# Hybrid decoder layer on one core: the mixed stage ordered by half steps and costs, two heads ahead, the softmax partly on ScalarE

## The reference

```python
def decoder_layer(x, ...):
    z = x @ w_in + b_in                      # u, q, k, v, two gates
    ssm = glu(gelu(s5_scan(u)))              # 32 groups, 64 states each
    att = attention(rope(q), rope(k), v) @ w_attn_up   # window 128, 8 heads, 2 kv heads, sinks
    mix = (sigmoid(g_ssm) * ssm + sigmoid(g_attn) * att) @ w_out
    x1 = layer_norm(ALPHA * x + mix)
    return layer_norm(ALPHA * x1 + peer(x1))

def peer(x):                                 # 8 heads, 16384 experts
    q = x @ peer_wq                          # per head two halves of 64
    v1, i1 = top_k(q[..., 0] @ k1.T, 16)     # 128 keys a side
    v2, i2 = top_k(q[..., 1] @ k2.T, 16)
    sc, sel = top_k(v1[:, None] + v2[None, :], 16)     # 16 of 256 sums
    idx, gate = (i1 * 128 + i2)[sel], softmax(sc)
    h = einsum('nhkd,nd->nhk', peer_u[idx], x)         # 128 rows of 1024 for each token
    return einsum('nhk,nhkd->nd', gelu(h) * gate, peer_v[idx])
```

## Time and profile before

| | us |
|---|---|
| median of 3 runs (lowest, highest) | 2155.72 (2154.64, 2161.78) |
| the profiled execution, and its span | 2155.55, span 2153.7 |
| first gather asked for | 346.0 |
| first dot product of tile 2 | 1033.75 |
| busy over the span: PE, DVE, POOL, ACT | 1588.6, 1368.6, 1335.9, 386.0 |
| mean granted TensorE clock | 0.88 of full speed |
| moved by DMA | 675.05 MB, 313 GB/s over the span |

### The profile page before, as it was taken

One profiled execution on the slowest core, in us unless ns is written; L12 is line 12 of the kernel. 1 busy time (PEld: TensorE's weight loads), 2 busy tenths in 40 slices (PEclk: granted clock), 3 DMA queues, 4 the chain that ended last, 5 costly groups with the idle time before them and its releaser, 6 DMA issues.

```text
span 2153.7 us, 16271 instructions
## 1 busy us (share of the span) xinstructions
PE 1588.6 (74%) x4705; PEld 794.3 (37%) x4705; DVE 1368.6 (64%) x3118; ACT 386.0 (18%) x905; POOL 1335.9 (62%) x1370
## 2 busy tenths in 40 slices
PE   6979986776987786876649676767658676777776
PEld 4667853443544433321224222223223222222222
DVE  7551237878999799758766675754648655444444
ACT  1222211123223222001111111111102121111111
POOL 0064004646686656676767777777777777777664
PEclk9979998868998898998879898889889898999889
DMA  5243335957899998999889999999999999999997
GB/s 216 88 82 115 135 115 208 374 196 282 315 401 378 385 343 308 373 356 346 297 342 351 358 378 347 377 365 381 356 389 344 351 362 388 377 356 397 350 361 294
DMA packets 186553, 675.05 MB, mean 313 GB/s; under 512 B 20961, under 2 KB 23441, under 8 KB 186049
## 3 DMA queue, kind: packets, MB, share of 16 engines
q0 software_dynamic: 167056, 609.25, 75.7%
q1 hardware_dynamic: 17632, 59.51, 7.7%
q10 hardware_dynamic: 1776, 5.24, 0.6%
HBM read 669.71 MB, written 3.69 MB: 313 GB/s over the span
## 4 chain that ended last, share of the span: by engine, by line
PE 29%; POOL 25%; DVE 16%; issue 15%; DMA 10%; another core or an unknown queue 3%; ACT 2%; SPq 0%; ACTq 0%; DVEq 0%; POOLq 0%
PE bank L812 12%; POOL region L525 9%; POOL wring L518 7%; PE bank L743 6%; POOL region L518 6%; DMA region<-in_pv,region 3%; PE bank L764 2%; DVE region L1238 2%; DMA wring<-in_pu,region 2%; DMA small<-in_pv,region 2%; POOL wring L525 1%; DVE wring L1238 1%; PE bank L564 1%; PE bank L783 1%
## 5 line engine op out<-in xcount | busy, mean ns | idle before, releaser
L812 PE MATMUL bank<-region,small 128*128 128x512 f32 (+1 forms) x1296 | 658.9, 653 | 293.4 <-ACT small L1482 146.3
L525 POOL DMA_INDIRECT region<-in_pv,region x392 | 441.5, 1126 | 219.7 <-issue 101.8
L812 PEld LDWEIGHTS bank<-region,small 128*128 128x128 f32 (+1 forms) x1296 | 247.7, 202 | 687.6 <-issue 530.9
L1238 DVE CUSTOM_DVE_ANT_0 wring<-wring,region 128x1024 f32<-128x1024 f32 x286 | 347.7, 1226 | 235.4 <-DMA wring<-in_pu,region 197.3
L1238 DVE CUSTOM_DVE_ANT_0 region<-region 128x1024 f32<-128x1024 f32 x290 | 353.1, 1226 | 189.2 <-DMA region<-in_pu,region 156.5
L518 POOL DMA_INDIRECT region<-in_pu,region x290 | 324.0, 1117 | 210.8 <-DVE region L1197 91.5
L518 POOL DMA_INDIRECT wring<-in_pu,region x286 | 300.7, 1051 | 95.3 <-issue 85.6
L1482 ACT ACTIVATE small<-small,region 128x128 f32<-128x128 f32 (+1 forms) x480 | 155.4, 387 | 652.3 <-DVE region L1212 294.3
L812 PE MATMUL bank<-discretisation,small 128*128 128x512 f32 (+1 forms) x196 | 111.1, 695 | 104.4 <-issue 53.3
L812 PE MATMUL bank<-wring,small 128*128 128x512 f32 x256 | 123.4, 615 | 24.4 <-issue 17.2
L743 PE MATMUL bank<-xT,wring 128*128 128x192 f32 (+1 forms) x512 | 130.5, 416 | 0.0
(11 more groups left out here) (246 smaller groups left out, 1712.7 us busy)
## 6 DMA issues: line engine op xcount, KB each, us to landing
wring<-in_w SPq DMA_DIRECT2D x102, 512.0 KB, 4.3
region<-in_pv,region POOLq DMA_INDIRECT x392
region<-in_pu,region POOLq DMA_INDIRECT x290
wring<-in_pu,region POOLq DMA_INDIRECT x286
out_y<-region ACTq DMA_DIRECT2D x4, 512.0 KB
small<-in_small ACTq DMA_DIRECT2D x1, 1669.0 KB, 14.3
xT<-in_xT SPq DMA_DIRECT2D x1, 1536.0 KB, 20.1
region<-in_x SPq DMA_DIRECT2D x3, 512.0 KB
```

The costliest lines, as they stand in the source:

```text
L525: pool.indirect_dma_start(ring_v[v_at.place[q]], None, io["pv"], bass.IndirectOffsetOnAxis(ind[:, k:k + 1], 0)).then_inc(g_v[v_at.place[q] ...
L812: last = mm(bank[6 + hf][0:tn, :], diag[:, d % DIAGS, 0:tn], ring_v[v_at.place[q]][:, 512 * hf:512 * hf + 512], start=k == 0, stop=t not i ...
L1238: V.tensor_tensor_reduce(out=ring_u[u_at.place[q]], in0=ring_u[u_at.place[q]], in1=x1[t], scale=1.0, scalar=0.0, op0=ALU.mult, op1=ALU.add ...
```

## The change

The same computation in another order. (1) `schedule()` gives each kind of item a cost on VectorE and TensorE (`COST`) and places the entries of the mixed stage by accumulated cost over the first 176 slots (`SPREAD`), between single slots; tile 0's entries have their own places at slots 50 to 112. A `peer` item is a *half step* of two slots (GELU stays at four). The same walk decides which V rows VectorE adds: those at which its summed load is under TensorE's. By my reading of the costs these are 62 rows of 192, six of them among the first 48. (2) Tile 1's choices are heads 0-1, 2-3 and 4-7. The queries of heads 0 and 1 are computed for tile 1 alone (`wqf`) before tile 0's norm, and for tile 0 later (`wql`); their two weight blocks are loaded ahead into two V places. (3) Items are split: gates into `gs` and `ga`, `wo` by halves with the norm as `ln`, `choose` into `choose` and `index`, the softmax into `s` and `p`, and `pt` apart from `pv`. VectorE and ScalarE do the mixer's items one half step later (`behind_next_step`). (4) The subtraction becomes the exponential's bias and the scaling a copy with a scale, head by head on ScalarE; a second buffer holds the other kv head's scores. (5) GpSimd's requests of V run on over a tile's end, and lag 6 slots in tiles 1 and 0; before slot 72 there are seven U places instead of eight. (6) SP's stop for slot 72 and the loads of x stand at the sixth gate's block.

```diff
-U_PLACES = ([0, 1, 2, 3, 4, 5, 10, 11], [0, 1, 2, 3, 10, 11], [0, 1, 2, 3] + list(range(6, 12)))
+U_PLACES = ([0, 1, 2, 3, 4, 5, 10], [0, 1, 2, 3, 10, 11], [0, 1, 2, 3] + list(range(6, 12)))
 V_PLACES = ([0, 1, 2, 3, 4, 5, 6, 7, 8], [0, 1, 2, 3, 4, 5], [0, 1, 2, 3, 4, 5] + list(range(9, 15)))
-V_LAG = 4
-V_SHARE = {1: [1] * 3 + [3] * 3 + [6] * 10, 0: [6] * 3 + [3] * 2 + [0] * 3}
-TOPS_AT = (9, 10, 12, 14, 16, 18, 20, 22, 24, 25)
-LATE_AT = 1
+V_LAG = {1: 6, 0: 6, 2: 4, 3: 4, 4: 4}
+SPREAD = 176
+CHOSEN_FROM, CHOSEN_TO = 50, 112
+COST = {"top": (5.0, 0), "choose": (4.6, 0), "index": (5.0, 0), "sc": (0, 2.5), "s": (4.1, 1.0), "p": (2.8, 0), "pt": (0, 1.4),
+        "pv": (0.4, 1.6), "qkv": (2.4, 10.3), "turn": (0, 1.2), "gs": (0, 5.5), "ga": (0, 5.5), "merge": (2.2, 8.2), "wo": (0.7, 7.0),
+        "ln": (6.2, 0), "xt": (0, 1.3), "wq": (0.3, 5.5), "fold": (0, 0), "wait": (4.0, 0)}
+DOT, V_BY_VECTOR, V_BY_TENSOR = 1.31, 1.29, 1.95
 DIAGS = 8
 STEP_SLOTS = 4
+HALF_STEP = 2
+CHOICES = {1: [(0, 2), (2, 4), (4, 8)]}
+AHEAD = 2
+AHEAD_PLACES = 7
...
+    s += [("wo", 1, 0), ("wo", 1, 1), ("ln", 1), ("wo", 0, 0), ("xt", 1)] + [("wqf", h) for h in range(AHEAD)] + [("sc", 1, 0), ("wo", 0, 1)]
+    s += [("top", 1, 0), ("top", 1, 1), ("choose", 1, 0), ("index", 1, 0), ("ln", 0), ("xt", 0)] + [("wql", h) for h in range(AHEAD)]
+    s += [("wq", 0, 2), ("wq", 0, 3), ("sc", 1, 1)] + [("wq", 0, h) for h in range(4, 8)]
...
+    cost = lambda entry: sum(sum(COST[i[0]]) for i in entry)
+    rate = sum(cost(e) for e in mix + tops) / SPREAD
+    slots, placed, d_load, p_load, on_vector = 0, 0.0, 0.0, 0.0, set()
+    for t in ORDER[:2]:
+        for c in range(n_slots(t) // HALF_STEP):
             s.append(("peer", t, c))
             if c == 0 and t != ORDER[0]:
+                s.append(("final", ORDER[0]))
+                d_load += 8.7
+            for k in range(HALF_STEP * c, HALF_STEP * c + HALF_STEP):
+                slots += 1
+                d_load += DOT
+                entries = []
+                if tops and slots >= CHOSEN_FROM + (CHOSEN_TO - CHOSEN_FROM) * (12 - len(tops)) // 11:
+                    entries.append(tops.pop(0))
+                while mix and placed + sum(map(cost, entries)) + cost(mix[0]) / 2 <= rate * slots:
+                    entries.append(mix.pop(0))
+                for entry in entries:
+                    placed += cost(entry)
+                    d_load += sum(COST[i[0]][0] for i in entry)
+                    p_load += sum(COST[i[0]][1] for i in entry)
+                    s += entry
+                if k and d_load + V_BY_VECTOR < p_load + V_BY_TENSOR:
+                    on_vector.add((t, k))
+                    d_load += V_BY_VECTOR
+                else:
+                    p_load += V_BY_TENSOR
+        s.append(("last", t))
...
+def behind_next_step(items, kinds):
+    out, held, begun = [], [], False
+    for item in items:
+        begun = begun or item[0] == "peer"
+        if begun and item[0] in kinds:
+            held.append(item)
+        elif item[0] == "peer":
+            out += [item] + held
+            held = []
+        elif item[0] in ("last", "final"):
+            out += held + [item]
+            held = []
+        else:
+            out.append(item)
+    return out + held
...
+            asked = 0
+            for q in range(len(on_dve)):
+                u_row(q)
+                while asked + V_LAG[place(asked)[0]] <= q:
+                    v_row(asked)
+                    asked += 1
+            for q in range(asked, len(on_dve)):
+                v_row(q)
...
-            def softmax(n, scores, sink, width, st):
-                mx, ex, sm, rs = (stat[:, 8 * i:8 * i + width] for i in range(4))
+            def softmax_begin(scores, sink, width, st):
+                mx, ex = (stat[:, 8 * i:8 * i + width] for i in range(2))
                 step(V.tensor_reduce(mx, scores, AX, ALU.max))
                 step(V.tensor_tensor(mx, mx, sink, ALU.max))
                 step(V.tensor_tensor(ex, sink, mx, ALU.subtract))
-                V.tensor_tensor(scores, scores, mx.unsqueeze(2).broadcast_to([128, width, st]), ALU.subtract).then_inc(scored, 1)
+                V.tensor_scalar(mx, mx, -1.0, None, ALU.mult).then_inc(scored, 1)
+            def softmax_end(n, scores, width, st):
+                ex, sm, rs = (stat[:, 8 * i:8 * i + width] for i in range(1, 4))
                 dve.wait_ge(expd_s, n)
                 step(V.tensor_reduce(sm, scores, AX, ALU.add))
                 step(V.tensor_tensor(sm, sm, ex, ALU.add))
-                step(V.reciprocal(rs, sm))
-                V.tensor_tensor(scores, scores, rs.unsqueeze(2).broadcast_to([128, width, st]), ALU.mult).then_inc(probs, 1)
-                dve.wait_ge(probs, n)
+                V.reciprocal(rs, sm).then_inc(inverse_s, 1)
+                dve.wait_ge(inverse_s, n)
...
-                step(S.activation(stat[:, 8:8 + width], stat[:, 8:8 + width], ACT.Exp))
-                S.activation(scores, scores, ACT.Exp).then_inc(expd_s, 1)
+                S.activation(stat[:, 8:8 + width], stat[:, 8:8 + width], ACT.Exp)
+                for i in range(width):
+                    last = S.activation(scores[:, i, :], scores[:, i, :], ACT.Exp, bias=stat[:, i:i + 1])
+                last.then_inc(expd_s, 1)
+            def scaled(n, scores, width):
+                act.wait_ge(expd_s, n)
+                act.wait_ge(inverse_s, n)
+                for i in range(width):
+                    last = S.activation(scores[:, i, :], scores[:, i, :], ACT.Copy, scale=stat[:, 24 + i:25 + i])
+                last.then_inc(probs, 1)
...
-                if p == (1, "wo", 0):
+                elif p in ahead:
+                    wait_item(sp, ("ht",))
+                if p == (1, "gs", 5):
```

More of the change, by code:

```diff
@@ new lines, in schedule @@
+    for n in range(1, len(parts)):
+        attention.append([("pt", *parts[n - 1]), ("p", *parts[n])])
+        attention.append([("pv", *parts[n - 1])] + ([("s", *parts[n + 1])] if n + 1 < len(parts) else []))
+    attention += [[("pt", *parts[-1])], [("pv", *parts[-1])]]
+    mix = [first[0], attention[0], first[1], first[2], attention[1], first[3]]
+    first, attention = first[4:], attention[2:]
+    for n, entry in enumerate(attention):
+        mix.append(entry)
+        if n < len(first):
+            mix.append(first[n])
@@ new lines, in schedule @@
+        s.append(("last", t))
+    assert not mix and not tops
+    late = [("top", 2, h) for h in range(4, 8)] + [("choose", 2, 1), ("index", 2, 1)]
+    for t in ORDER[2:]:
+        nxt = [("sc", t + 1, 0), ("sc", t + 1, 1)] + [("top", t + 1, h) for h in range(4)] + [("choose", t + 1, 0), ("index", t + 1, 0)]
+        nxt += [("top", t + 1, h) for h in range(4, 8)] + [("choose", t + 1, 1), ("index", t + 1, 1)]
+        for c in range(n_slots(t) // HALF_STEP):
+            s.append(("peer", t, c))
+            if c == 0:
+                s.append(("final", ORDER[ORDER.index(t) - 1]))
+            if late and c >= 2 and c % 2 == 0:
@@ L125, in mixer_first @@
             held = item
-            out.append(("before", *item[1:]))
         else:
@@ L532, in _ @@
-                for k in range(ns - V_LAG, ns):
-                    v_row(k)
+                for p, (h0, h1) in enumerate(choices(t)):
+                    if t and k == TOPK * h0:
+                        pool.wait_ge(idx_s, chosen(t, p))
+                if u_at.before[q] is not None:
+                    pool.wait_ge(dots, u_at.before[q] + 1)
+                elif u_at.place[q] == 10:
+                    pool.wait_ge(filled, plan.filled[plan.last_use[[p for p in pieces if not p[0] and slot_of[p] == 6][-1]]])
+                elif u_at.place[q] == 11:
+                    pool.wait_ge(filled, plan.filled[("pt", 3, 1, 1)])
```

394 lines of the change are left out of this document (216 added, 178 removed).

## The result

The changed kernel is slower. In runs on one chip it takes 2185.61 us (median of 4 runs, 2179.59 to 2195.67), the kernel before 2158.75 (4 runs, 2154.64 to 2164.22): ratio 1.0139, 95 % interval 1.0094 to 1.0185. Forecast were 2088 us and a gain. The profiled execution took 2180.1 us, span 2177.9.

A forecast was written before the change was run, and what follows sets the result against it. The last three tiles were taken as a gather stream only fewer bytes could shorten, so the change could move only tile 2's first dot. 318 + 179 + 221 + 254 + 1116 = 2088 us, 67 less; range 2050 to 2135.

The forecast's parts named there:

- First gather at 312, first dot at 318: Start of tile 1: two heads searched and chosen ahead, first gather at about 312 instead of 346 us, first dot 318.
- Slots 0 to 47, 179 us: First 48 slots: 145 us of VectorE work, 18 of start waits, a tenth lost; 179 instead of 199 us.
- A V row then sits unused for two slots less: Tiles 1 and 0, V lag six: freed V places against one U place less; nothing taken for either.
- Slots 48 to 111, 221 us: 80.7 MB at 381 GB/s are 212 us; 221 taken, bounds 206 and 240, instead of 206.6.
- Slots 112 to 191, 254 us: Rows and 17 blocks at 375 GB/s are 247 us; 254 taken, bounds 247 and 277, instead of 277.
- a named wait of 10 us: End of the mixed stage: GpSimd's 9.95 us idle until tile 2's indices are written goes, indices due by slot 176.
- Tiles 2 to 4, 1116 us: Last tiles: V requests run over the tile's end, 6 us less; 1116 us, bounds 1108 and 1135.
- The wait of the final norm: Later tile boundaries: norm waits some 8 us longer, covered by ten U places; uncovered, 8 us at each of two boundaries.
- TensorE as the bound: Rival 3, mixed stage: 34 more V rows on TensorE; 2125 us at clock 0.87, 2170 at 0.80; slower has chance 0.09.
- Slots 48 to 191 over 500 us: Sign that the prediction is wrong: these slots take over 500 us with TensorE over 90 % busy.
- TensorE over 90 % busy: Second half of that sign: TensorE over 90 % busy while slots 48 to 191 take over 500 us.
- as coupled as now: Rival 1, mixed stage: only the head start is kept, stage stays at 334 GB/s, ends 34 us earlier; 2121 us, chance 0.14.

The follow-up runs named there:

- lag, drain and spread mended: Changed kernel with V lag of four, tile 0's second output projection drained just before its norm, entries over 190 slots instead of 176 (also called the fastest version): 0.9951.
- Taking work away: Changed kernel, tiles 1 and 0, with half of each V product's columns (TensorE): 1.0054; half of each dot product's elements (VectorE): 1.001; both: 0.9963.
- lag four and moved drain: Changed kernel with V asked for four slots behind U and tile 0's second output projection drained just before its layer norm: 1.0038 of the kernel before.
- the wider spread: Entries over 190 slots instead of 176: alone on the changed kernel 1.0171; with V lag of four and tile 0's second output-projection drain just before its norm 0.9951.
- the old share: 96 of 192 V rows on VectorE instead of 62, on the version with lag, drain and spread mended: 1.0047.
- half the work on both engines: Changed kernel with half the columns of V products on TensorE and half the elements of dot products on VectorE in tiles 1 and 0: 0.9963.
- the mends: Changed kernel with V lag of four and tile 0's second output projection drained just before its norm: 1.0038; with entries over 190 slots too: 0.9951.
- V lag of four: Changed kernel with V requested four slots behind U in tiles 1 and 0 instead of six: 1.0102 of the kernel before on the same chip.

## Why the prediction was wrong, point by point

- **First gather at 312, first dot at 318** (321.3, 326.1). The parts were right (two searches and a choice of two heads from 304.1 to 320.4, 16.3 us against 9.9 + 7.3). What failed is the claim that the search follows the scores: VectorE's in-order queue had a drain of later TensorE work ahead of it, 7 us. With it moved the gather is at 314 to 315, the first dot at 320 to 321. The item list, which was there to be read, showed it.
- **Slots 0 to 47, 179 us** (187.4). VectorE's work was forecast at 145 us and was 139; its waits were larger. With lag, drain and spread mended it is 172.
- **"A V row then sits unused for two slots less... I take nothing for either."** This step weighed the wrong two things. The places that the lag frees are real (V waits 79.0 to 23.4 us) and brought no time, and one U place less cost nothing (0.9997). What it left out is that the later request makes VectorE wait for V rows (12 to 45 us) and, in a circle, GpSimd for dot products (30.5 to 157). The nothing in the sum was nearly right all the same, because these waits took the place of others: 0.4 % in the kernel before, at the edge of its interval, and 0.3 to 0.5 % in the changed one, inside the intervals.
- **Slots 48 to 111, 221 us** (235.3; 229.2 in the fastest version, within the bounds 206 to 240). More TensorE work was foreseen, a pace of 381 GB/s was not reached: 327 GB/s, and 342 in the fastest version. VectorE waited 21 us for TensorE here, before not at all.
- **Slots 112 to 191, 254 us** (299.1). The largest error, and the step that failed. I divided the bytes by 375 GB/s, which puts the engines' waits for each other at nothing, and removed a named wait of 10 us. The wait did go (1.30 us before tile 2's first dot), the pace was never there: 307 GB/s, DMA share 0.85. The old order ran here at 334 GB/s with VectorE's longest wait 3.5 us; the new one has waits of 9.6 to 13.9 us at drains and V rows. In sum VectorE is idle for 92 us instead of 54, and 34 of these are waits for TensorE, which were 0. Its slots 144 to 167 hold the queries' blocks and 16 of VectorE's V rows, and take 101 us instead of 67. No edit mended the stretch: 284 to 316 us in all versions of the new order that compute everything. Taking work away gives 8 us (TensorE), 16 (VectorE), 24 (both).
- **Tiles 2 to 4, 1116 us** (1132.2, before 1121.8). Six us less were forecast for requests that run over the boundary. The changed kernel's slots 192 to 255 took 199 and 200 us, before 192. Versions with lag four and moved drain took 186 to 189, but 200 with the wider spread and the old share on top, and two versions with lag six took 191 and 192. So these slots show no effect of the requests either way. The same instructions took 1098 to 1133 us from tile 2's first to the last dot, so most of the 16 us can't be assigned. The wait of the final norm, priced at 8 us, shows as 15.3 and is covered.
- **The rivals.** TensorE as the bound was to decide below a clock of 0.82; the stages show 0.86 to 0.95, and still it was slower. "Slots 48 to 191 over 500 us" came true (534), "TensorE over 90 % busy" did not (430 of 534, 80 %). At the mean clock of 0.90 these 430 us are an estimated 387 at full clock, against the rival's 401: the work was sized well, and the waits, put at a tenth, were a fifth. The rival that the coupling eats more than the head start brings was missing: apart from TensorE as the bound, I had let the stage stay "as coupled as now" at worst. The chance of 0.09 for slower rested on that bound, so it is no credit to the forecast that slower was among the outcomes.

What stays open: why the last stretch doesn't fall below 274 us with half the work on both engines. Left are the serial chain (last merges, output projection, norm, queries, scores, search), in which TensorE stands for the norm and then VectorE for the queries, and the fixed order in which VectorE meets it; no run separated these two. Also open is why the wider spread pays only behind the mends: the two kernels that show it differ in lag and drain both. That late V rows use up the slack it makes fits (38 us of waits for them in slots 112 to 191, against 9), but was not tried by itself.

## What to carry to other kernels

With in-order engines, look for each moved item at what stands ahead of it in *every* engine's list, before summing busy times; here that was 7 us at once. A request put later to free a buffer moves the wait to the one who uses the data, and here it only took the place of another wait of the same engine: a large wait in a profile is no price until a run without it is faster. The sum of an engine's idle time, by what ended it, says more than one row; here it pointed at the handovers from TensorE, which no single edit removed. A stretch at 99 % DMA share is a result of an order, not a property of the stage: don't multiply bytes of a new order by it. And an edit can gain only in company (the spread), so mend the others before judging it.

## What the runs showed of the hardware

Chips differ in the gather stream. On one of them the last tiles ran at 1035 to 1048 us instead of 1098 to 1133, all four kernels tried on it alike, and the kernel before took 2076.47 us on it against 2157 to 2172 in the other five groups of runs. From 1700 to 1900 us, first that chip (V lag of four), then the usual (changed kernel), GB/s in 40 slices of 5 us:

```profile
GB/s 410 410 410 407 407 408 409 408 406 411 410 410 331 306 340 377 375 327 412 415 406 411 405 406 410 409 406 410 410 408 408 410 412 404 410 407 410 410 410 408
```

```profile
GB/s 347 394 341 401 412 407 410 410 410 410 411 311 178 320 360 385 392 394 393 312 379 418 410 409 418 351 325 290 395 417 409 409 410 409 410 409 412 347 135 343
```

Both reach 410 GB/s; the usual chip has dips to 135 to 180 that the other has not (373 against 399 GB/s over the 200 us). In the two deepest dips ScalarE and GpSimd wait at once for a releaser that shows as "remote"; at 1217 us even VectorE does, within a search (6.7 us at L1282). These waits set the chips apart: summed over all engines they are 0 in each of the four traces of that chip, and 153 to 265 us in each of the sixteen others, the kernel before included (246). What stops the engines isn't shown, nor that it makes up the whole difference.
